# First stage: modulation products in column lanes, an earlier first weight chunk; last stage: four second rows added by VectorE and the normalisation in another order

## What is computed

```python
mod = SiLU(c) @ w_ada + b_ada            # 9 rows (1 prompt, 8 samples) x 6*1024
sh1, sc1, g1, sh2, sc2, g2 = split(mod)
h = x * (1 + sc1) + sh1
q, k, v, u, gates = split(h @ w_in)      # 1024 -> 5632 columns
...                                      # attention, pooling, w_out, layer norm, h2
y = top-2 of 16 experts for each token (HierMoE(h2))
out = LN(alpha * x1 + (1 + g2) * y) * ln2_g + ln2_b
```

## Time and profile before

| | us |
|---|---|
| median of 3 runs | 1418.38 |
| lowest, highest run | 1416.62, 1418.63 |
| profiled execution | 1416.77 |
| its span | 1414.8 |
| first stage, up to the barrier | 67.9 |
| last stage, from the barrier | 1352.7 to 1414.8 |
| PE busy | 1304.4 (92% of the span) |
| DVE busy | 992.3 |

### The profile page before, as it was taken

One profiled execution on the slowest core, in us unless ns is written; L12 is line 12 of the kernel. 1 busy time (PEld: TensorE's weight loads), 2 busy tenths in 40 slices (PEclk: granted clock), 3 DMA queues, 4 the chain that ended last, 5 costly groups with the idle time before them and its releaser, 6 DMA issues.

```text
span 1414.8 us, 24706 instructions
## 1 busy us (share of the span) xinstructions
PE 1304.4 (92%) x8846; PEld 1113.3 (79%) x8846; DVE 992.3 (70%) x1502; ACT 742.3 (52%) x1321; POOL 129.8 (9%) x95
## 2 busy tenths in 40 slices
PE   6799999999999999999999997999389999999955
PEld 2488899999899898998999984877278887888821
DVE  1423548667586775867758667599779998999837
ACT  1324433454454544545545545423348998999724
POOL 1423210000000000000000000000011111111051
PEclk9889999999999999999999998999669999999987
DMA  9598333233332333323333243463177999556875
GB/s 316 178 289 284 96 118 107 80 86 90 108 90 78 86 90 110 93 73 86 97 104 98 83 139 101 148 210 134 74 283 259 349 318 364 187 199 208 280 208 185
DMA packets 210979, 229.42 MB, mean 162 GB/s; under 512 B 17942, under 2 KB 184794, under 8 KB 210747
## 3 DMA queue, kind: packets, MB, share of 16 engines
q1 hardware_dynamic: 195627, 173.39, 39.4%
q0 software_dynamic: 6976, 25.23, 5.5%
q10 hardware_dynamic: 8280, 29.51, 5.2%
HBM read 173.07 MB, written 46.79 MB: 155 GB/s over the span
## 4 chain that ended last, share of the span: by engine, by line
PE 75%; DVE 9%; DMA 5%; ACT 5%; issue 2%; SPq 2%; POOL 1%; ACTq 0%; DVEq 0%; POOLq 0%
PE AB L990 11%; PE AB L994 11%; PE AB L991 11%; PE S L917 6%; PE S L919 6%; PE S L918 6%; PE S L1088 4%; ACT F L1493 3%; PE T L1114 3%; PE OB L917 2%; DMA F<-in_b_ada 1%; PE OB L918 1%; PE OB L919 1%; PE S L932 1%; DMA F<-y_d,slot 1%
## 5 line engine op out<-in xcount | busy, mean ns | idle before, releaser
L1493 ACT ACTIVATE R<-F 128x1024 fp32r<-128x1024 f32 (+4 forms) x305 | 292.5, 1006 | 85.6 <-DVE F L2071 45.7
L990 PE MATMUL AB<-R 128*128 128x344 f32 x960 | 315.1, 332 | 1.2 <-ACT F L1493 1.2
L991 PE MATMUL AB<-R 128*128 128x344 f32 x960 | 303.9, 320 | 0.0
L917 PE MATMUL S<-R 128*128 128x512 f32 x480 | 192.2, 400 | 1.8 <-ACT F L1493 1.6
L919 PE MATMUL S<-R 128*128 128x512 f32 x480 | 187.9, 391 | 0.0
L918 PE MATMUL S<-R 128*128 128x512 f32 x480 | 187.5, 391 | 0.0
L990 PEld LDWEIGHTS AB<-R 128*128 128x128 f32 x960 | 181.3, 189 | 4.8 <-issue 4.7
L991 PEld LDWEIGHTS AB<-R 128*128 128x128 f32 x960 | 181.5, 189 | 1.7 <-issue 1.7
L1493 ACT ACTIVATE F<-AB 128x344 f32<-128x344 f32 (+3 forms) x129 | 59.1, 460 | 216.6 <-PE AB L994 195.5
L994 PE MATMUL AB<-R 128*128 128x344 f32 x960 | 171.6, 320 | 0.0
L994 PEld LDWEIGHTS AB<-R 128*128 128x128 f32 x960 | 155.5, 188 | 0.0
(11 more groups left out here) (289 smaller groups left out, 2217.3 us busy)
## 6 DMA issues: line engine op xcount, KB each, us to landing
F<-in_w_ada SPq DMA_DIRECT2D x24, 1024.0 KB
F<-in_w_in SPq DMA_DIRECT2D x44, 512.0 KB, 4.1
F<-in_w_e_gate SPq DMA_DIRECT2D x16, 1024.0 KB
F<-in_w_e_up SPq DMA_DIRECT2D x16, 1024.0 KB
F<-in_w_e_down SPq DMA_DIRECT2D x16, 1024.0 KB, 9.1
y_d<-F ACTq DMA_DIRECT2D x32, 512.0 KB
out<-F SPq DMA_DIRECT2D x24, 512.0 KB, 4.1
F<-F SPq DMA_DIRECT2D x192, 43.0 KB, 1.9
```

The costliest lines, as they stand in the source:

```text
L917: mm(out, w[0], m[1], start=start, stop=False)
L990: mm(bank[:, 0:PIECE], whl[b][0][:, k, :], x[1][:, k, :], start=(k == 0), stop=False)
L991: mm(bank[:, 0:PIECE], whl[b][0][:, k, :], x[0][:, k, :], start=False, stop=False)
L1493: return nc.scalar.activation(out, in_, func, **kw)
```

## The change

In the first stage:

- PE's `ada` takes the form of `late`: 32 matmuls of 9 x 64 in four column lanes instead of 8 of 9 x 256. DVE's `ada_sum` becomes four sums of 9 x 64.
- The sample tokens are turned by PE behind the second burst, into another part of bank OB. The product with 1 + scale1 stands before the last burst on DVE, the sum behind it.
- The sums for `lam` stand before the last burst on DVE. ACT's Exp, `w_split(0)` and POOL's `w_rest(0)` stand between pieces 11 and 12 of h.
- SP issues the first chunk of `w_in` before chunk 8 of `w_ada`, and chunk 10 of `w_ada` before the barrier instead of behind it.

In the last stage:

- Tiles 2 and 3 get a buffer for the second row too (in R), both rows are gathered plainly, and DVE adds them. All eight gathers of tiles 0 to 3 come first, then the first rows of tiles 4 to 6.
- On ACT, `squared(t-1)` stands before `total(t)` instead of behind it, squares what is in PSUM, and a Sqrt of one element heads the stage.
- On DVE, the first product of `affine5` becomes `centred5(t)`, right behind the mean of the tile and ahead of ACT's root; the rest of `affine5(t-2)` stands ahead of `mean5(t-1)`.

```diff
-    yb, g2s = [at(16096), at(20192)], at(13024)
+    yb, g2s = [at(16096), at(20192)] + [R[:, D * i:D * i + D].bitcast(F32) for i in range(2)], at(13024)
...
+            wchunk(UC, 0)
             ada(EARLY)
             ada(EARLY + 1)
...
-            wchunk(UC, 0)
+            ada(EARLY + 2)
...
             wchunk(UC + P, 1)
-            ada(EARLY + 2)
...
             for k in range(KC):
-                last = mm(bank[0:9, 0:AW], sTc[:, k, :], adaw[ABUF[n]][:, k, :], start=(k == 0), stop=(k == KC - 1))
+                for j in range(LANES):
+                    last = mm(bank[32 * j:32 * j + 9, 0:LW], sTc[:, k, :], adaw[ABUF[n]][:, k, LW * j:LW * j + LW],
+                              start=(k == 0), stop=(k == KC - 1), skip_group_check=True)
...
+            if n == 4:
+                for k in range(KC):
+                    last = tr(OB[:, 64 + NS * k:64 + NS * k + NS], xr[0:NS, NT, k * P:(k + 1) * P], ident[0:NS, 0:NS])
+                last.then_inc(cT_done, 1)
...
-        pe.wait_ge(modT_copied, 8)
-        for k in range(KC):
-            last = tr(OB[:, NS * k:NS * k + NS], xr[0:NS, NT, k * P:(k + 1) * P], ident[0:NS, 0:NS])
-        last.then_inc(xT_done, 1)
...
+        for m in range(16):
+            h_hi_part(m)
+            if m == 11:
+                act.wait_ge(lam_sum, 1)
+                act_(lamt[:, 0:2], lamt[:, 2:4], ACT.Exp).then_inc(lam_exp, 1)
+                w_split(0)
...
-            mark(TT(modrow[ABUF[n]][0:9, 0:AW], bank[0:9, 0:AW], badab[ABUF[n]][0:9, 0:AW], ALU.add), ada_row, n + 1)
+            for j in range(LANES):
+                cols = slice(LW * j, LW * j + LW)
+                last = TT(modrow[ABUF[n]][0:9, cols], bank[32 * j:32 * j + 9, 0:LW], badab[ABUF[n]][0:9, cols], ALU.add)
+            mark(last, ada_row, n + 1)
...
+            if m == 11:
+                w_rest(0)
...
-            act_(WB[t % 3][0:rows, :], x5[t][0:rows, :], ACT.Square, bias=nmean5[t % 3][0:rows, :], accum_out=square5[t % 3][0:rows, :]).then_inc(square_done.sem, 1)
+            act_(WB[t % 3][0:rows, :], WB[t % 3][0:rows, :], ACT.Square, bias=nmean5[t % 3][0:rows, :], accum_out=square5[t % 3][0:rows, :]).then_inc(square_done.sem, 1)
...
+        act_(rstd5[0], const("eps"), ACT.Sqrt)
+        total(0)
+        for t in range(1, NT + 1):
+            squared(t - 1)
             total(t)
...
-            if t < 2:
+            if t < 4:
                 V(TT(y, y, yb[t], ALU.add))
...
+        def centred5(t):
+            rows = P if t < NT else NS
+            x = x5[t][0:rows, :]
+            mean_done.wait(dve, t + 1)
+            V(STT(out=x, in0=x, scalar=nmean5[t % 3][0:rows, :], in1=l2g[0:rows, :], op0=ALU.add, op1=ALU.mult))
...
+            if t >= 2:
+                affine5(t - 2)
             if 1 <= t <= NT + 1:
                 mean5(t - 1)
-            if t >= 2:
-                affine5(t - 2)
+                centred5(t - 1)
...
-        for t in range(2):
+        for t in range(4):
             gather5(t, 0, ya[t])
             gather5(t, 1, yb[t])
-        for t in range(2, 5):
+        for t in range(4, 7):
             gather5(t, 0, ya[t])
-        for t in range(2, NT + 1):
+        for t in range(4, NT + 1):
             y5_landed[t].wait(pool, 16)
             gather5(t, 1, ya[t], compute_op=ALU.add)
```

More of the change, by code:

```diff
@@ L1501, in h_hi_part @@
             act_(hT[0][:, m // 2, 512 * (m % 2):512 * (m % 2) + 512], h32[m % 2]).then_inc(h_hi, 1)
-        for m in range(16):
-            h_hi_part(m)
-        act.wait_ge(hs_ready, 1)
-        act_(hT[0][:, :, SEQ:T], hs32).then_inc(h_hi, 1)
-        act.wait_ge(lam_sum, 1)
-        act_(lamt[:, 0:2], lamt[:, 2:4], ACT.Exp).then_inc(lam_exp, 1)
-        act.wait_ge(h_hi, 17)
         def w_split(g):
@@ L2089, in _ @@
                     h_part(m)
-        mod_columns(EARLY - 1)
-        for m in range(12, 16):
-            h_part(m)
-        dve.wait_ge(xT_done, 17)
-        V(TT(hs32, OB[:, 0:64].rearrange("p (k b) -> p k b", k=8), modT[:, 8:16, 1:9], ALU.mult))
-        mark(TT(hs32, hs32, modT[:, 0:8, 1:9], ALU.add), hs_ready, 1)
-        dve.wait_ge(h_hi, 17)
-        V(TT(hT[1][:, :, SEQ:T], hs32, hT[0][:, :, SEQ:T].bitcast(F32), ALU.subtract))
         dve.wait_ge(ld_small, 16 * 8)
@@ L2102, in _ @@
         mark(rsum(lamt[:, 2:4], lamv[:, 0:2, :]), lam_sum, 1)
+        mod_columns(EARLY - 1)
+        dve.wait_ge(cT_done, 2)
+        V(TT(hs32, OB[:, 64:128].rearrange("p (k b) -> p k b", k=8), modT[:, 8:16, 1:9], ALU.mult))
+        for m in range(12, 16):
+            h_part(m)
+        mark(TT(hs32, hs32, modT[:, 0:8, 1:9], ALU.add), hs_ready, 1)
         dve.wait_ge(lam_exp, 1)
@@ L2604, in affine5 @@
             std5.wait(dve, t + 1)
-            V(STT(out=x, in0=x, scalar=nmean5[t % 3][0:rows, :], in1=l2g[0:rows, :], op0=ALU.add, op1=ALU.mult))
             V(nc.vector.reciprocal(r, r))
```

24 lines of the change are left out of this document (12 added, 12 removed).

## The result

| | before | after |
|---|---|---|
| median | 1417.5 (4 runs, 1416.21 to 1418.63) | 1399.01 (4 runs, 1396.31 to 1401.51) |
| profiled execution | 1416.77 | 1400.47 |
| its span | 1414.8 | 1398.6 |

The ratio is 0.9869, with a 95% interval from 0.9846 to 0.9893: 18.5 us less by the medians, 16.3 by the two profiled executions. The prediction said 1396.0, with 1390 to 1403 as its range, and 22.4 us less. The time lies 3.0 us above the forecast and in the range; the gain is 17% smaller than the sum.

What follows compares the result with a forecast made beforehand. The prediction took PE to bound the kernel, with 75% of the chain. Gains of 10.6 in the first stage, 5.3 behind the barrier and 6.5 in the last stage made 22.4 us: 1418.4 to 1396.0, range 1390 to 1403.

Steps and rivals of the forecast that it cites:

- First stage: Up to the first barrier: it opens at 57.3 instead of 67.9, 10.6 us earlier, bounds 7 to 13.
- The mechanism of the lanes: First-stage chunk products in column lanes: 2.5 us less PE time a chunk, four DVE sums costing 0.9.
- The first period: First to second DVE burst: DVE sets the pace, 6.85 us against 10.6; 1.2 us set against for half clock.
- The third period: Between the third and last DVE bursts: 7.05 us instead of 7.74, with the sums of `lam` inside, gaining 0.7.
- The tail: From the last burst's start to the first barrier: 8.5 us instead of 12.1, small DVE instructions running beside POOL; 3.6 won.
- PE's list: PE's first-stage work is through earlier: chunk 9 lands at about 52.5 and its product ends at 54.
- Rival one: First stage becomes bound by loads and keeps only about 5 of the 10.6 us; time 1401.6, chance 0.10.
- Behind the barrier: Two pieces and chunk 10's product take 11.1 us instead of 16.4; 5.3 won, bounds 2 to 6.5.
- The last stage: Plain gathers for two tiles give 2.9 us, a tail of 8.1 instead of 11.75 gives 3.6; together 6.5, bounds 4 to 8.
- Rival two: Last stage stays bound by gathers at 4.8 us a tile, only the tail's 3.6 stay; 1398.9, chance 0.08.
- Rival three: Each of 14 switches between lanes and whole array on PE costs up to 0.23 us, 3 us; 1399, chance 0.04.
- Rival four: PE enters the pieces at half clock and stays there, 3.1 us more a piece; 1433, chance 0.03.

Runs made afterwards that it cites:

- e12: Changed kernel with w_ada chunks 0 to 7 multiplied by the whole array again and summed by one DVE instruction; median 1406.5, ratio 0.9941 to before.
- e1: Changed kernel with the 1 MB rope table loaded behind chunk 8 of w_ada, two chunks later; median 1398.9, ratio 0.9881 to before.
- e3: Changed kernel with DVE's small instructions moved out of the tail behind the last burst; median 1399.3, ratio 0.9879 to before.
- e5: The changed kernel measured once more, nothing altered; median 1398.9, ratio 0.9886 to before.
- e6: Changed kernel with the rope table loaded behind chunk 16 of w_ada, some 40 us later; median 1397.2, ratio 0.9874 to before.
- e7: Changed kernel with rope 40 us later, chunk 11 ahead, small DVE instructions out of the tail, w_in split behind the last burst; median 1395.3, ratio 0.9860 to before.
- e8: Changed kernel with chunk 10 of w_ada issued behind the barrier again; median 1402.9, ratio 0.9907 to before.
- e9: Kernel before with the changed kernel's last stage, nothing else; median 1410.5, ratio 0.9980 to before.
- e10: Kernel before with only the last stage's plain gathers of tiles 2 and 3 and DVE's two sums; median 1415.8, ratio 1.0011 to before.
- e11: Kernel before with only the last stage's new orders on ACT and DVE; median 1414.5, ratio 0.9998 to before.
- e4: Changed kernel with chunk 11 of w_ada issued ahead of the state table, w_pool and third w_in chunk; median 1398.6, ratio 0.9890 to before.
- e2: Changed kernel with the split of the first w_in chunk, on ACT and POOL, back behind the last burst; median 1397.4, ratio 0.9871 to before.

## Why the prediction was right, and which terms were wrong

**First stage, forecast 10.6, measured 6.1.** This is below the bounds named for it, 7 to 13. The sum went through three periods, from burst to burst, to a last burst at 48.8; it began at 51.64.

- *The mechanism of the lanes held*: sums 0.91, period 6.99 from 36.21 to 43.20 (forecast 6.85), and e12 puts their worth, less the gap of the next item and the wait for `lambda` that it does not have, at 6.2 us of burst start, against 7.0 forecast.
- *The first period* was 8.74. Its step said that DVE would be what is waited for. It is not where the chunk's product is late, and here PE stood 1.35 us inside the product, between the 63rd and the last matmul (the trace counts 64 for the 32 of the code), waiting for nothing that the profile shows. The product had also begun 0.32 late, for chunk 4's load. The kernel before had such a gap too, of 1.82 us in the samples' transposes. The forecast removed that one with the transposes it sat in; it came back elsewhere, and the last section says how regularly. Its cause stays open. The first burst itself began 0.75 later than before, of which the half clock (1.11 for four transposes instead of 0.66) is 0.45. The 1.2 us set against both together was too little.
- *The third period* was 8.44 instead of 7.05: `lambda` by DMA, 1.32. The step that failed is the order of the loads. The forecast moved the sums of `lam` ahead on DVE and costed them at 0.85, but their loads stand behind 1 MB of rope on SP's list. e1 shows it: without the megabyte ahead the wait is gone.
- *The tail*, forecast 8.5, measured 10.2. The detour over POOL was sized well (`h_part(14)` 5.14 us behind the burst's start, forecast 4.5; the 0.67 is ACT's wait for `w_in`). What failed is the sentence that the six small instructions run beside POOL. The first of them lasted until POOL was through at 60.47, and the rest ran one after the other behind it, to 61.46; DVE's low part of the samples ended at 61.72. e3 moves them out of the tail and wins 1.2.
- *PE's list*: in the forecast chunk 9 lands at about 52.5 and its product ends at 54. In after PE waited for the load until 58.18, and the product ended at 60.08, 6 us later than forecast, at half clock. That was hidden behind DVE. But as the chunk landed in this trace, it would have held the barrier at 60.1 with DVE on time, 2.8 us above the forecast 57.3; somewhat less, since a faster DVE would also have freed the chunk's buffer earlier. e1 came within 0.2 us of this limit. The product ended at 59.0 to 60.1 in e1 to e5, and at 58.0 and 57.3 in e6 and e7, where the rope is out of the queue.

Rival one, the stage bound by loads, thus came true in good part. The forecast said against it that the DMA engines have room, at a share of 0.64; up to 58 us it was 0.90. Its named case, the first chunk of `w_in` later than 49, happened (it landed at 52.0, 8.71 us after its issue) and cost 0.67; the load that cost more was a small one that the rival did not name, and the one that would have been the limit was chunk 9.

**Behind the barrier, forecast 5.3, measured 4.4.** Piece, product and piece took 10.6 us (11.1 forecast, 16.4 before), without a wait for chunk 10 and at full clock from the middle of the first piece on. The forecast worked out that chunk 11 would land about 12 us behind the barrier where PE wants it after 11.1, and kept 5.3 all the same. It landed at 11.8, PE wanted it at 10.6, and waited 1.16. The step that failed is the last one, to set its own result aside. By e8 3.0 to 3.4 of the 4.4 are chunk 10's; the rest I did not take apart. The 4.4 also leans on the one trace of before: in e9, e10 and e11, with before's code there, this stretch is 34.9 to 36.1 us instead of 36.9, against 32.4 and 33.2 in after and e5.

**The middle**: no change expected and none found.

**The last stage, forecast 6.5, measured 5.9 (e5 6.8, e9 4.4).** The tail of 8.1 was 7.8; the orders alone (e11) win 4.0 in it and lose 0.4 ahead of it. For the gathers the forecast wrote 2.9 as if it stood by itself. Alone it is 0.6 (e10), because ACT's `total` ahead of `squared` and its table load then end last. The two alone make 4.2, both together 6.5 to 7.4 in the eight traces without waits for gathers. So the sum is right and its division is not. How much of this is the two parts needing each other, and how much the waits of the execution, is not settled: e9, with 2.65 us of such waits, has 4.4. The forecast had no wait at tiles 5 and 6; its gathers landed 2 us or more ahead of DVE.

**Rivals two to four.** Rival two had the last stage bound by gathers, at 4.8 us a tile; waits of 0.27 to 1.81 us at two tiles, in three of eleven traces, are a trace of it. Rival three: in after a chunk's product starts at 40.33, 0.22 behind the start of the transposes of the row at 40.11, which takes 0.29, so nothing is seen to wait between the two forms. The Trainium skill, "TensorEngine Tiling (Array Packing)", Key Properties, says that a change of tiling mode drains TensorE; at this grain the trace shows no price for it. Rival four, half clock that stays: PE did enter the pieces at half clock (its four transposes at 52.51 took 1.12) and was at full clock from 65.4 on.

The net of the errors: 4.5 too much in the first stage, 0.9 behind it, 0.6 at the end and 0.3 in the middle make 6.2 by the profiled executions. The medians leave 3.9 of it, since the profiled execution of after was 1.5 us above its median and that of before 0.7 below. That is luck: by the profiled executions the forecast was 1394.4 and the measured time 1400.5. All four errors point the same way, and the range held because it was 13 us wide, not because each term was known that well.

## What to carry to other kernels

- When a stage in front of a barrier gets shorter, look at what is issued only behind the barrier. Here chunk 11 was issued about 4 us after it and, where PE waited for it, came 12 to 13 us after it. Three kernels (e1, e3, e6) opened the barrier 1.6 to 2.0 us earlier and none reached the double product earlier; with the load moved forward in the list (e4, e7) it came earlier.
- An instruction that is moved forward takes its operands' loads with it: check where in the queue those stand, the small ones too.
- An engine that stands just behind the critical path limits the gain. Ask for each engine when it would be through, and not only for the one that ends last now (chunk 9's product, 60.08).
- Two edits that attack two waits of the same engine need not add up. Measure each alone and together before a sum is divided among them, and more than one execution of each: waits of 1.5 to 2.7 us came and went in one and the same stage.

## What the runs showed of the hardware

**DVE beside POOL.** A DVE sum of one element per partition took 2.35 us while POOL ran an instruction of 2.35 (e2), and another 0.95 (after, 0.16 alone); one of 128 x 64 took 0.83 instead of 0.23. Each ended within 0.1 us of the end of POOL's running instruction. All of these have both operands in SBUF. The chunk sums at 47.88, with one operand in PSUM, took 0.91 for four beside POOL's low parts (47.54 to 49.68), which is their price alone. The Trainium skill, "SBUF — State Buffer", section "Who interferes with whom", says that a DVE instruction with two SBUF inputs contends with a GpSimd instruction that reads SBUF, that the contention is an exclusive lock, and that the order of issue decides who is blocked. The rows agree with it, in time and in which operands are hit. It also names tensor-scalar instructions in a two-port mode; the one of 128 x 8 in e3 took 1.25 instead of 0.17, to the end of POOL's instruction, while those of 128 x 1 took 0.15 to 0.27. The forecast's tail would have been 1.2 us longer, had it gone by this.

**The clock behind a wait.** These are waits of PE for a chunk behind the barrier, and the product behind them, which takes 1.08 at 2.4 GHz and 1.90 at 1.2 GHz. After 1.16 us 1.08 (after), after 1.83 us 1.08 (e8), after 2.12 us 1.90 (e9), after 2.24 us 1.63 (e1), after 2.31 us 1.33 (e6), after 2.42 us 1.80 (e10), after 2.56 us 1.90 (before), after 2.66 us 1.85 (e7), after 4.18 us 1.90 (e3). But after 2.31 us it was 1.08 in e11, and the clock did not fall:

```profile
76.13 1.08 PE L973 MATMUL S<-F 128*9 128x64 f32 x64 [2.31 <-DMA F<-in_b_ada]
```

So in this stretch no wait of 1.83 us or less was followed by a fall, seven of the eight of 2.12 or more were, and the length of the wait alone does not decide it. Where the clock fell in e1, e3, e6 and e7, it was 1.3 to 2.4 us more up to the next chunk.

**A gap that stays at its place.** PE stood 1.35 us inside a product of 64 small matmuls (after), 1.82 inside transposes (before), each time with nothing that the profile shows as its reason. The other traces tell that it is tied to a place in the program. In all nine traces with the lanes it stands ahead of the last matmul of chunk 4's product, with 349 matmuls of the trace ahead of it, and takes 0.86 to 1.41 us. In the four with the old first stage (before, e9, e10, e11) it stands behind the first of the samples' transposes, with 345 ahead of it, and takes 1.82 to 2.03. e12 has none of half a microsecond. In each of the thirteen a packet of 16 KB on the DMA queue of kind `instruction` (in after from 32.38 to 33.52) ended 1.20 to 1.50 us before PE went on. In e12 such a packet runs from 64.70 to 65.90, while PE waits for DVE. This speaks for the loading of instructions, but other packets of that queue have no gap behind them (in after those at 37.63 and 43.50), and no run changed it, so the cause is not shown.
